# A three-layer transformer kernel on one core: y tiles ahead of the last gates, and four small moves

## The reference

```
# first block: window attention, 32 heads of 64, 4 key/value heads, a sink per head
h = rmsnorm(x, g_pre);  q, k, v, z = split(h @ w_in)
p = softmax([q k^T / 8 - slope * distance inside a window of 128, sink]);  o = p v
x = x + rmsnorm((o * silu(z)) @ w_out, g_post)
# second block, layers l = 0, 1
h = rmsnorm(x, pre_norm_g[l]);  q_lat, kv_lat, k_pe, gb, gc, xin, q_mem, gate = split(h @ w_in[l])
a = softmax attention of 8 heads over projected latents, with rope on 64 of the 192 columns
c = gb * conv3(gc * xin);  m = attention over 256 memory tokens, 4 heads
x = x + rmsnorm((concat(a, c, m) * silu(gate)) @ w_o[l], post_norm_g[l])
```

## Time and profile before

| | us |
|---|---|
| three runs | 2237.65, 3156.2, 2236.09; median 2237.65 |
| the profiled execution | 2233.37 |
| its span on the core | 2231.6 |
| PE busy | 2199.5 |
| DVE busy | 1365.8 |
| ACT busy | 814.3 |
| POOL busy | 116.1 |

### The profile page before, as it was taken

How to read it: one execution, slowest core, us unless ns; L and a number is a source line. 1 busy time by engine, 2 the same in 40 slices (tenths; PEclk the granted TensorE clock), 3 DMA queues, 4 the chain that set the end, 5 groups by cost and what they waited for, 6 DMA issues and landing times.

```text
span 2231.6 us, 27542 instructions
## 1 busy us (share of the span) xinstructions
PE 2199.5 (99%) x10348; PEld 1823.5 (82%) x10348; DVE 1365.8 (61%) x1952; ACT 814.3 (36%) x1232; POOL 116.1 (5%) x151
## 2 busy tenths in 40 slices
PE   8999999999999999999999999999999999999998
PEld 7888888878888888888888788888888888888787
DVE  6677888773248543567677632385434677677665
ACT  6343333442234421334333422344212443335221
POOL 0100011001110100000000011101000000000000
PEclk9999999999999999999999999999999999999999
DMA  7445444452237222225444432373222143434432
GB/s 278 172 151 163 154 160 141 157 169 97 97 141 268 95 95 94 76 76 160 133 134 127 149 127 94 127 263 109 100 99 73 64 156 130 140 117 154 167 119 108
DMA packets 89852, 303.05 MB, mean 136 GB/s; under 512 B 7408, under 2 KB 48624, under 8 KB 66480
## 3 DMA queue, kind: packets, MB, share of 16 engines
q1 hardware_dynamic: 83760, 271.33, 36.1%
q10 hardware_dynamic: 4608, 16.78, 2.0%
q0 software_dynamic: 1408, 13.89, 1.7%
HBM read 253.74 MB, written 48.23 MB: 135 GB/s over the span
## 4 chain that ended last, share of the span: by engine, by line
PE 92%; DVE 4%; ACT 2%; DMA 1%; issue 1%; POOL 0%; SPq 0%; ACTq 0%; DVEq 0%; POOLq 0%
PE acc L542 70%; PE sc L542 10%; PE ov L542 5%; DVE lo L1355 2%; ACT hi L992 2%; PE ov L701 1%; PE sc L688 1%; PE sc L687 1%; PE sc L883 1%; PE sc L882 1%; DMA area<-memT_dram 0%; DMA g<-xT_dram 0%; PE acc L561 0%; PE acc L558 0%; PE acc L557 0%
## 5 line engine op out<-in xcount | busy, mean ns | idle before, releaser
L542 PE MATMUL acc<-h_hi,hi 128*128 128x512 f32 x2240 | 881.1, 393 | 18.6 <-DVE h_lo L1424 8.3
L542 PE MATMUL acc<-h_lo,hi 128*128 128x512 f32 x2240 | 873.7, 390 | 0.0
L542 PE MATMUL acc<-h_hi,lo 128*128 128x512 f32 x2240 | 873.1, 390 | 0.0
L1355 DVE TENSOR_TENSOR lo<-raw,hi 128x2048 fp32r<-128x2048 f32 (+2 forms) x194 | 427.2, 2203 | 398.4 <-ACT hi L992 391.4
L992 ACT ACTIVATE hi<-raw 128x2048 fp32r<-128x2048 f32 (+2 forms) x194 | 358.2, 1846 | 472.5 <-PE acc L542 311.2
L542 PEld LDWEIGHTS acc<-h_hi,hi 128*128 128x128 f32 x2240 | 421.5, 188 | 114.9 <-issue 15.8
L542 PEld LDWEIGHTS acc<-h_hi,lo 128*128 128x128 f32 x2240 | 421.3, 188 | 88.4
L542 PEld LDWEIGHTS acc<-h_lo,hi 128*128 128x128 f32 x2240 | 421.6, 188 | 86.4 <-issue 1.4
L999 ACT ACTIVATE sq<-acc 128x512 f32<-128x512 f32 x32 | 19.2, 600 | 230.4 <-PE acc L542 223.5
L1067 ACT ACTIVATE prob<-prob,st 128x256 f32<-128x256 f32 x128 | 63.6, 498 | 108.2 <-DVE st L1485 108.2
L542 PE MATMUL sc<-hi,h_hi 128*128 128x512 f32 (+1 forms) x160 | 59.4, 371 | 2.6 <-DVE lo L1355 2.6
(11 more groups left out here) (291 smaller groups left out, 2815.6 us busy)
## 6 DMA issues: line engine op xcount, KB each, us to landing
raw<-w_dram SPq DMA_DIRECT2D x170, 1024.0 KB, 4.7
turned<-pt SPq DMA_DIRECT2D x32, 512.0 KB, 3.2
pt<-turned SPq DMA_DIRECT2D x64, 256.0 KB, 5.1
turned<-pt SPq DMA_DIRECT2D x32, 448.0 KB, 3.0
pt<-turned SPq DMA_DIRECT2D x64, 224.0 KB, 4.0
xr<-residual ACTq DMA_DIRECT2D x16, 512.0 KB, 5.1
residual<-g ACTq DMA_DIRECT2D x16, 512.0 KB, 4.7
raw<-w_dram SPq DMA_DIRECT2D x8, 896.0 KB, 6.0
```

Source lines behind the costliest of these rows:

```text
L542: ins = pe.matmul(to, a, b, start=first and n == 0, stop=last and n == 2)
L1355: dve.tensor_tensor(lo[c.slot][:, 0:width], raw[c.slot][:, 0:width], hi[c.slot][:, 0:width].bitcast(F32), ALU.subtract).then_inc(lo_done, 1)
```

## The change

Five parts.
- **Tiles of y, first block.** ACT makes high tiles 0 to 4 before the tanh of A, and the split of the second output chunk and tanh B follow tiles 5 to 7. DVE makes low tiles 0 to 11 between the steps of the two gates; y_14 (its two halves apart) stands between tiles 9 and 11, y_15 before tile 14. PE does scores B two k-tiles sooner in z_a.
- **Tiles of y, second block.** In both layers ACT makes 7 high tiles instead of 5 before the last gate's tanh, and the split of the second output chunk comes before tile 7. DVE makes 6 low tiles instead of 5 before the last gate is multiplied, and `y_head` of the last head comes just before tile 15 in both layers (before tiles 14 and 12 until now).
- **Last queries.** The scaled query of B is made between DVE's two turns of A.
- **Angles.** They come one chunk pair later in the output product.
- **Norm factors.** The wait for the gain row moves from before the loop of the last product's chunks to chunk 5, where the row is first used.

```diff
@@ -121,7 +121,7 @@
     SQUARES = (10, 11, 12, 13, 8, 9, 14, 15, 0, 1, 2, 3, 4, 5, 6, 7)
     FIRST_SQUARES = SQUARES[:2]
     STORE_FIRST, STORE_LAST = (5, 6), (4, 7, 0, 1, 2, 3)
-    EARLY = 5
+    EARLY, AHEAD = 5, 7
     SPLIT_AT = (0, 1, 3, 4, 6, 7, 9, 10)
     def sq_no(l, which):
@@ -715,7 +715,7 @@
                 pair(i, False)
             features(q_a, h_hi, h_lo)
             features(q_b, h_hi, h_lo, meanwhile=[(6, lambda: scores_first(A)), (10, lambda: values_first(A - 1))])
-            features(z_a, h_hi, h_lo, meanwhile=[(12, lambda: scores_first(B))])
+            features(z_a, h_hi, h_lo, meanwhile=[(10, lambda: scores_first(B))])
             features(z_b, h_hi, h_lo, meanwhile=[(3, lambda: values_first(A))], last_reader=True)
             def high(c, k, first):
@@ -1095,34 +1095,28 @@
             q_hi(B, q_b)
             exps_first(B)
             split(wo_first)
+            def early_y_hi_tiles(gates, tiles=EARLY):
+                act.wait_ge(h_half_read, gates)
+                for t in range(tiles):
+                    y_hi_tile(t)
+            act.wait_ge(x_stored, 16)
+            act.wait_ge(y1, A + 1)
+            early_y_hi_tiles(1)
             tanh_first(A, z_a)
-            def early_y_hi_tiles(gates):
-                act.wait_ge(h_half_read, gates)
-                for t in range(EARLY):
-                    y_hi_tile(t)
-            def y_hi_tiles(nxt, last_ready, weights_at=KT, weights=None):
-                for t in range(EARLY, KT // 2):
-                    y_hi_tile(t)
-                split(nxt)
-                for t in range(KT // 2, KT - 1):
-                    if t == weights_at:
-                        weights()
-                    y_hi_tile(t)
-                last_ready()
-                y_hi_tile(KT - 1)
-            act.wait_ge(x_stored, 16)
-            act.wait_ge(y1, EARLY + 1)
-            early_y_hi_tiles(1)
+            for t in range(EARLY, KT // 2):
+                y_hi_tile(t)
+            split(chunk2(0, WO + 1))
             tanh_first(B, z_b)
-            act.wait_ge(y1, PAIRS)
             act.wait_ge(chunk_done, N1)
-            y_hi_tiles(chunk2(0, WO + 1), lambda: act.wait_ge(y1, PAIRS + 1))
+            for t in range(KT // 2, A):
+                y_hi_tile(t)
+            for t in (A, B):
+                act.wait_ge(y1, t + 2)
+                y_hi_tile(t)
             def reload_residual(l, w):
                 slot = w % XR
@@ -1312,7 +1306,8 @@
                                        bias=nm[:, b:b + 1], accum_out=ls[:, b:b + 1]).then_inc(exp2, 1)
                     if last:
                         split(chunk2(l, N2 + WO))
-                        early_y_hi_tiles(l + 2)
+                        act.wait_ge(y_b, l * MLA + MLA - 1)
+                        early_y_hi_tiles(l + 2, AHEAD)
                     else:
                         split(chunk2(l, HEAD + 3 * j + 3, i, 6), HW[1 - j])
                         split(chunk2(l, HEAD + 3 * j + 4, i, 6))
@@ -1327,11 +1322,16 @@
                 head(MLA // 2 - 1, 0)
                 head(MLA // 2 - 1, 1, last=True)
+                split(chunk2(l, N2 + WO + 1))
                 act.wait_ge(y_b, l * MLA + MLA)
+                y_hi_tile(AHEAD)
                 act.wait_ge(y_a, l * MLA + MLA)
-                act.sem_inc(waited, 1)
-                y_hi_tiles(chunk2(l, N2 + WO + 1), lambda: act.wait_ge(y_a, l * MLA + (MLA + 1)),
-                           WEIGHTS_AT[l], lambda: pt_high(l * MLA + MLA))
+                for t in range(AHEAD + 1, KT - 1):
+                    if t == WEIGHTS_AT[l]:
+                        pt_high(l * MLA + MLA)
+                    y_hi_tile(t)
+                act.wait_ge(y_a, l * MLA + (MLA + 1))
+                y_hi_tile(KT - 1)
             def row_squares(cg):
                 for b in range(TB):
@@ -1484,7 +1484,7 @@
                     dve.tensor_scalar(es[:, part], mx[:, part], -1.0, sink, ALU.mult, ALU.add)
                     dve.tensor_scalar(nm[:, part], mx[:, part], -1.0, None, ALU.mult).then_inc(shift1, 1)
-            def softmax_back(i):
+            def softmax_back(i, meanwhile=None):
                 for par in range(2):
@@ -1501,26 +1501,34 @@
                     dve.transpose(pt1[:, 0:T1].rearrange("p (a n s i) -> p n s a i", a=QUADS, n=2, s=SEEN)[:, par],
                                   prob1[:, par * 1024 + P:(par + 1) * 1024].rearrange("p (s a j) -> p s a j", s=SEEN, a=QUADS))\
                         .then_inc(turned1, 1)
+                    if par == 0 and meanwhile is not None:
+                        meanwhile()
+            def y_half(i, par):
+                rows_ = HALVES[par]
+                return dve.scalar_tensor_tensor(g[rows_, tile(i)], ov[par][rows_, :], 0.5, sg[rows_, :], ALU.mult, ALU.mult)
             def y_first(i):
                 dve.wait_ge(values1, i + 2)
                 dve.wait_ge(sg_done, i + 1)
-                for par in range(2):
-                    rows_ = slice(HD * par, HD * par + HD)
-                    ins = dve.scalar_tensor_tensor(g[rows_, tile(i)], ov[par][rows_, :], 0.5, sg[rows_, :], ALU.mult, ALU.mult)
-                ins.then_inc(y1, 1)
-            def q(i, qc):
+                y_half(i, 0)
+                y_half(i, 1).then_inc(y1, 1)
+            def q_scaled(qc):
                 dve.wait_ge(chunk_done, qc.n + 1)
                 dve.scalar_tensor_tensor(qt[:, :], acc[qc.slot][:, :], HD ** -0.5, r_x[:, :], ALU.mult, ALU.mult)\
                     .then_inc(evacuated[qc.slot], 1)
+            def q_low(i):
                 dve.wait_ge(q_hi_done, i + 1)
                 for par, half_ in enumerate(HALVES):
                     ins = dve.tensor_tensor(q1[HALVES[1 - par], tile(par)], qt[half_, :], q1[half_, tile(par)].bitcast(F32),
                                             ALU.subtract)
                 ins.then_inc(q_split, 1)
+            def q(i, qc):
+                q_scaled(qc)
+                q_low(i)
             def gate_first(i, zc, meanwhile=None):
                 dve.wait_ge(chunk_done, zc.n + 1)
@@ -1556,32 +1564,50 @@
             split(z_a)
             softmax_front(A)
             y_first(A - 1)
-            softmax_back(A)
-            q(B, q_b)
+            softmax_back(A, lambda: q_scaled(q_b))
+            q_low(B)
             split(z_b)
             softmax_front(B)
             softmax_back(B)
             split(wo_first)
-            gate_first(A, z_a)
-            y_first(A)
-            for t in range(EARLY - 1):
+            def y_while_a():
+                for t in range(3):
+                    y_lo_tile(t, t + 1)
+            def y_while_b():
+                for t in range(4, 10):
+                    y_lo_tile(t, t + 1)
+                dve.wait_ge(values1, A + 2)
+                y_half(A, 0)
+                y_lo_tile(10, 11)
+                y_half(A, 1).then_inc(y1, 1)
+                y_lo_tile(11, 12)
+                dve.wait_ge(y1, A + 2)
+            gate_first(A, z_a, y_while_a)
+            dve.wait_ge(sg_done, A + 1)
+            y_lo_tile(3, 4)
+            gate_first(B, z_b, y_while_b)
+            for t in (12, 13):
                 y_lo_tile(t, t + 1)
-            gate_first(B, z_b, lambda: y_lo_tile(EARLY - 1, EARLY))
+            y_first(B)
+            for t in (A, B):
+                y_lo_tile(t, t + 1)
+            split(chunk2(0, WO + 1))
             def y_lo_tiles(before, nxt, last, split_at=KT, weights_at=KT, weights=None):
-                for t in range(EARLY, KT):
+                for t in range(AHEAD - 1, KT):
                     if t == split_at:
                         split(nxt)
                     if t == weights_at:
                         weights()
-                    if t == max(KT - 4, weights_at % KT):
+                    if t == KT - 1:
                         last()
                     y_lo_tile(t, before + (t + 1))
                 if split_at == KT:
                     split(nxt)
-            y_lo_tiles(0, chunk2(0, WO + 1), lambda: y_first(PAIRS - 1))
             def m_normed_pair(l, w):
                 for n in range(2):
@@ -1615,17 +1641,21 @@
             def output(l):
+                def both(i):
+                    split(chunk2(l, WO + 1, i, 2))
+                    m_normed_pair(l, i + 1)
+                    split(chunk2(l, WO + 2, i, 2))
+                    m_lo_pair(l, i - 1)
                 split(chunk2(l, WO + 2))
                 dve.wait_ge(memory_in, l * 16 + 16)
                 m_normed_pair(l, 0)
                 m_normed_pair(l, 1)
+                both(1)
                 if l == 0:
                     angles()
-                with dve.Fori(1, KT // 2 - 1) as i:
-                    split(chunk2(l, WO + 1, i, 2))
-                    m_normed_pair(l, i + 1)
-                    split(chunk2(l, WO + 2, i, 2))
-                    m_lo_pair(l, i - 1)
+                with dve.Fori(2, KT // 2 - 1) as i:
+                    both(i)
```

(7 more changed lines are left out.)

## The result

| | before | changed | ratio |
|---|---|---|---|
| runs, median (us) | 2237.34 (4: 2236.09, 2237.02, 2237.65, 3156.2) | 2219.18 (4: 2218.25 to 2219.78) | 0.9918, 95% interval 0.9906 to 0.9930 |
| profiled execution: span | 2231.6 | 2217.4 | |
| PE, first to last matmul begun | 2215.75 | 2200.92 | |

One run of the kernel before took 3156.2 us, 41% above its others; the median without it is 2237.02. The change took 18.2 us off (16 to 21 by the interval) where 13.5 were predicted: 5 us under the 2224 forecast, at the low end of the range. It is under 2%, as foreseen; but the interval is 0.24% wide, so a change much smaller than 2% can be told from none here.

The account below looks back on a forecast made before the run. PE, busy 99% of the span, was taken to bound the kernel, so only its stops could be won: 6.6 + 4.0 + 2.9 = 13.5 us off 2237.65, forecast 2224, range 2219 to 2234.

Parts of the forecast that it names:

- the term of the last product: Before the last product, moving DVE's wait for the gain row removes one PE stop: 2.9 us.
- 2237.65, is 4.3 above it: 2224.1 on that scale: Whole kernel: 2219.9 us from the profiled execution, shifted by the median's distance of 4.3 us to 2224.1.
- First block, 6.6: First block to its output product: 7.3 us of stops and clock less 0.7 lost at values A.
- The 7.3 booked for the stops and the clock: First block to output product: four PE stops worth 5.6 us plus 1.7 us of lower clock behind the first.
- price: At values A, the query between the turns delays the copies of probabilities by 0.69 us: 0.7 us lost.
- third rival: At values A, the 1 MB load pushes the copies, stopping PE up to 7 us; gain 5 to 9; 6%.
- The fourth stop: In the first block's output product near 507, PE's wait for a split behind the angles goes: 0.86 us idle.
- Layer 0, 4.0: Layer 0 to its output product: three stops worth 4.2 us go, less 0.2 of new waits: 4.0 us.
- The 0.2 booked for nil margins: At layer 0, low tiles 6 to 8 come barely in time: 0.2 us of wait.
- second rival: Near 468, the 1.7 us of lower clock belong only to some executions: gain 11.8 us, total 2226; 10%.
- fourth rival: Whole kernel: a PE that never rests gets a lower clock; at 1% lower, about 2242 us; 2%.
- Rivals 1, 3 and 5: 1: late tile handovers, gain 7 to 10 us, 25%; 5: another engine or fetch stops PE, 2236 to 2239, 3%.

Follow-up runs that it names:

- e1: The kernel before, run again with no edit: median 2237.28 us, ratio 1.000.
- e3: The kernel before with only the second block's y tiles in the new order: 2232.94 us, ratio 0.9983.
- e5: The kernel before with only the angles one chunk pair later: 2235.41 us, ratio 0.9995.
- e7: The changed kernel with the wait for the gain row back before the last product's chunks: 2225.41 us.
- e4: The kernel before with only the first block's y tiles in the new order, queries and scores of B as before: 2233.23 us, ratio 0.9985.
- e2: The kernel before with only the wait for the gain row moved to chunk 5: 2231.06 us, ratio 0.9977.
- e12: The changed kernel with B's query scaled twice between DVE's turns and scores of B before k-tile 12: 2219.31 us.
- e8: The changed kernel with B's scaled query behind both turns again and scores of B before k-tile 12: 2219.82 us.
- e9: The changed kernel with the gain row's wait early again and the last x pieces' loads held back until the gain rows landed: 2222.21 us.
- e6: The changed kernel with the angles before the first chunk pair again: 2223.05 us.
- e11: The changed kernel with the second block's y tiles in the old order: 2222.92 us.
- e10: The changed kernel with the gain row's wait only one split behind its old place, before the split of chunk 3: 2218.83 us.

## Why the forecast was right in kind and too small
**Which work bounds it: right.** Every stop named in the prediction is gone and none took its place. The two traces alone differ by 7.65 + 4.24 + 2.93 = 14.8 us at the three places, against the 13.5 of the sum; PE's first matmul came 0.67 later, so that the profiled execution took 2219.24, where the prediction had 2219.9 "for its like".

**The step that failed: the term of the last product, "2.6 + 0.26 = 2.9 us", and with it "2237.65, is 4.3 above it: 2224.1 on that scale".** The prediction took the stop at the gain row from one execution, and carried the distance between that execution and the median over unchanged, as if it lay in work that the change leaves alone. Most of it lay in the term of 2.9 us itself. The stop at the gain row was 2.6 us in that execution, and 3.66 to 4.77 in four of the five other traces that have it untouched (e1, e3, e5, e7; 2.80 in e4), with seven to ten matmuls at the lower clock behind each of those four: 1.4 to 2.0 us. Measured alone the term is 5.9 (e2) or 6.2 (e7): **3.0 to 3.3 of the 4.7 us that were missing**. The changed kernel has nothing of the kind: its median, 2219.18, and its profiled execution, 2219.24, are the same, where before they lay 4.3 apart. Not all of those 4.3 need be this wait: the first 300 us took 0.3 to 2.7 us more in e1 to e5 than in the first trace, and no run separates that from the medians.

**That the result lies inside the range is luck.** The range took its high end from the median (2237.65 less 4) but its low end from the profiled execution (2233.37 less 14.4). From the median the largest gain considered would have given 2223.3, above every run of the changed kernel. No rival had a gain above the forecast.

**First block, 6.6: too small by 1.05.** The 7.3 booked for the stops and the clock came, and the "price", 0.7 for values A, "a delay passes through whole", did not: PE reached values A 0.19 us sooner than before, and e12 put 0.71 us more in the same place and saw 0.13. The reason shows in the landing of the last of the four copies: 6.2 to 6.5 us in all seven traces with the query behind both turns (before, e1 to e5, e8), 4.3 to 5.1 in six of the seven with it between them. The seventh, e9, had 6.4, and there PE did stop:
```profile
455.98 1.49 PEld L702 LDWEIGHTS ov<-pt,vcur 128*64 128x64 f32 x16 [1.49 <-DMA pt<-turned]
```
That cost 1.1 us, -6.51 in the table for -7.65, and so a little more than the edit is worth, 0.6 to 0.9 (e8). This is a stop of the kind that the third rival named, but far from its "up to 7"; a load that follows the copies closer cannot be its cause alone, since it followed as close in the six traces without the stop. That the "price" was nil is luck in this sense: the prediction allowed for it ("0, if the copies land as much quicker") but had no reason for it. Why the later copies land sooner is open; no run separated the copies from the load behind them, whose issue follows that of the last copy by 0.5 us now and by 1.5 before.

**The fourth stop was priced at its present length.** 0.86 idle + 0.26 is right for the angles alone (e5: 1.13). With the first three stops gone it would have been 2.1 to 2.2 plus the clock (e4, e6), 3.9 us in the runs. The sum was right because the change does both; anyone who had done only the first part would have got 3.7 us and not the 5.5 booked for it.

**Layer 0, 4.0: right**, 4.24 in the trace, 4.0 and 3.7 in runs (e3, e11). The 0.2 booked for nil margins did not occur.

**Clock.** The second rival was about it: a lower clock at 468 in some executions only. That is so, and more was lost to it at the last product. The stops of 2 us and more, with what followed: 2.83 and 2.77 start to start (e2, e3) at 468 without a lower clock, 2.89, 2.94 and 3.06 (before, e1, e5) with; 2.63 and 2.53 at 503 (e4, e6) with; at the last product 3.02 and 3.19 (before, e4) without, 2.40 (e9) and the four of 4.05 to 5.16 with. The Trainium skill (TensorE: Matmul & The Clock Gate, Part 1 on the HAM clock gate) says that the cold stretch varies from run to run of one kernel; the traces agree, before and e1 being one kernel: behind its stops the lower clock came at one place (468) in the one and at three (14, 471, 2076) in the other. The fourth rival, a lower clock for an engine that never rests, is refuted: the mean clock of the changed kernel is 0.999, that of before 0.998.

**What adds up.** 7.65 + 4.24 (trace) + 5.9 to 6.2 (runs) = 17.8 to 18.1, for 18.2 measured. Rivals 1, 3 and 5 gave less than the forecast, and the result lies on the other side of it.

## What to carry to other kernels
A profiled execution that lies apart from the median is a question before it is a scale: look which of the waits to be removed ends on something that varies (a DMA among other DMAs, a clock behind a stop), and price it at its usual length, not at the one in the trace. Stops that follow one another on one chain are priced together: with the earlier ones gone, the later one grows by what the chain behind it did not gain (0.86 to 2.24 us here). Here a small load that one engine waited for landed sooner when the bulk loads behind it were held back (e9, 3.2 us); to let the wait stand one chunk later gave more (e10, some 6 us against e7) and cost nothing.

## What the runs showed that was not expected
- Four gain rows of 256 KB were asked for 0.5 to 0.6 us apart. The first three landed in 3.4 to 4.6 us in all traces; the last, which 1 MB loads follow, in 5.06 to 7.19 us, and with those loads held back in 4.44 (one trace).
- The last of the four copies of probabilities landed in 6.2 to 6.5 us in the seven traces of the old order. In the new one it was asked for 0.9 to 1.7 us later, and landed in 4.3 to 5.1 in six traces of seven. The cause is open.
- Behind a stop of 2.0 to 3.0 us of idle the granted clock fell in six of the ten places at 468, 503 and the last product, behind one of 3.66 or more in four of four; near 14 us it fell behind 2.06 and 1.86 (e1, e4) and not behind 1.71 (e5). Six to ten matmuls then begin 0.427 us apart and not 0.227.
- The first 300 us of the same instructions differ by up to 2.7 us between traces. Most of that is a wait near 14 us, up to 2.06 us of idle, and in e1 and e4 the lower clock behind it.
